# A two-block transformer kernel: shorter way to the first expert routing (columns, root, first head's query)

## The chip, the cores and the metric

One core of a Trainium2 chip runs the whole program. TensorE (PE), VectorE (DVE), ScalarE (ACT), GpSimd (POOL) and SyncE (SP) each run their own list of instructions in order and wait for each other through semaphores. The metric is the device time of one execution in microseconds (µs). TensorE has two clock levels, 1.2 and 2.4 GHz; the profile shows the granted level as a share of the full one, 0.5 or 1.

## What is computed

256 tokens of 1024 features go through two blocks. In the first, attention and a short convolution are mixed and added to x; then 8 heads route every token to 16 of 16384 experts each, and the rows of these experts are gathered from HBM. The second block is a hybrid attention and delta-rule layer. Cut to what the change touches:

```python
x = x + gt1 * (mixed @ w_out[l])
h2 = rmsnorm(x, ln_ffn_g[l]) * (1 + sc2) + sh2
x = x + gt2 * peer_ffn(h2, peer_wq[l], peer_keys[l], peer_u[l], peer_v[l])

# peer_ffn: 8 heads; queries against two sets of 128 keys, the best 16 of each side,
# then the best 16 of their 256 sums give 16 experts and 16 gates g a token
u = expert_u[ec]
act = jax.nn.gelu(jnp.einsum('cd,ced->ce', xc, u).astype(jnp.float32))
return jnp.einsum('ce,ced->cd', gc * act, expert_v[ec])
```

sh2, sc2 and gt2 are parts of the conditioning row `silu(c) @ w_mod + b_mod`.

## The kernel before

The 256 tokens are two tiles (`a` = 0, 1) of 128. All engines' programs are written out by hand: a straight front part, and then one common list of chores, made by `loop_chores`, that each engine walks through, doing its own share of every chore. So the order on every engine is fixed by where a chore stands in that list, and an engine that waits holds back all that stands behind.

Front part, near its end, for tile 0: `attn_mm` multiplies the mixed features with w_out; `attn_add` adds to X; VectorE's `q_norm1` sums the squares of X (L1538) and ScalarE's takes the root (L2110). `mod_cols` on TensorE turns weighted rows of w_mod into columns: the rows m = 0 to 3 are sh2 and sc2 (in RT and rowb), m = 6 and 7 are the second half's gate gt2, which is kept in the rowb row `R_G2`. Every column is a product with one output column, so each loads 128x128 weights for it. VectorE's `mod2` adds the bias. `conv_root(1)` is the root of the convolution's norm for tile 1: TensorE sums squares with ones (L963), ScalarE takes the root (L2191), VectorE's `conv_mix(1)` takes the reciprocal and scales (L1516, L1520). `q_norm2(0)` scales X (L1550, L1552), turns it (L815) and evacuates it with sc2 and sh2 to hT (L1405, L2128). `scores_mm(4)`, `scores_add(4)` belong to the attention of tile 1, whose softmax is spread over the gather. `q_project(0, 0, ..)` makes the queries of heads 0 and 1 from hT and the peer_wq slab (L1016), ScalarE copies them to mixT, `keys` multiplies them with the keys (L1040).

Then the chores. `route(0)` takes heads (0), (1), (2, 3), ... in this order. For each: `top8`, `drop8`, `top16`, `at8`, `at16` on VectorE find the 16 best of both sides, `cand` to `cat16` the best sums, `same`, `pick`, `total`, `expert` the expert numbers. `spread_i` and `spread_g` on TensorE (L1054) spread numbers and gates over the partitions, `take_i` and `take_g` on VectorE take them. `q_back` (L1031) turns hT back to token order for the dot products, and its results are copied to tok2 on ScalarE.

The gather: 128 steps p, two fetches each. One fetch is one indirect DMA from GpSimd (L2474), 268.45 MB in 256 of them, about 1.05 MB each, into one of 8 buffers of AR. At first the buffers 0, 1, 2, 3, 4 and 7 are free for it; every later fetch waits until `accumulate` (L1072) has used the data of its buffer. `dot` on VectorE (L1689) multiplies the first half of the row with the token, `weight` on ScalarE (L2221, L2223, L2106) takes gelu, gate and a diagonal, `accumulate` on TensorE adds the second half. Around them stand pieces of the rest: `scores_mm(5)`, `weigh(4)` (VectorE, L1439, needs ScalarE's exponentials of `scores_add(4)`), routing of the later heads, and for a = 1 the first tile of the second block. After the last fetch the second tile of the second block remains.

A PSUM bank is taken in rotation by `take`; with no event named it is held until `drop`. `S_WQ` are the two peer_wq slabs.

```python
def first_wait(a, h0):
    if h0 == 0:
        return [("idx", 0, 6), ("gwp", 0, 6)] if a else [("mod_cols2", 1)]
```

The first `top8` waits for all columns, since `drop8` writes into the scratch `sw`, which is the same memory as `R_G2`.

## Time and profile before

| | µs |
|---|---|
| median of 3 runs | 1291.72 |
| lowest and highest | 1291.27, 1292.57 |
| the profiled execution | 1300.05 |
| its span in the trace | 1298.2 |

| engine | busy µs | share |
|---|---|---|
| TensorE | 1094.3 | 84% |
| VectorE | 793.2 | 61% |
| ScalarE | 448.3 | 35% |
| GpSimd | 294.0 | 23% |

The profiled execution is 0.6% longer than the median. Shares are means over stages with different limits: a front part (to about 208 µs), the gather (to about 1000 µs) and the rest of the second block. A wait is put down to the event that came last.

### The profile page before, as it was taken

What the parts mean: (1) busy time and instruction counts of PE and PEld (TensorE: products, weight loads), DVE (VectorE), ACT (ScalarE), POOL (GpSimd) and SP (SyncE); (2) the same over time, 40 slices, a digit from 0 to 9 for tenths busy, and PEclk for the clock granted to TensorE, in tenths of its full rate; (3) what the DMA queues carried; (4) which work ended last, traced back from release to release, by engine and by line L of the source; (5) the groups of instructions that cost most, each with busy time, mean ns of one, the idle gap of its engine ahead of it and who ended that gap; (6) DMA issues with size and microseconds to landing.
All of it is one profiled execution on the core that took longest, in us unless ns stands there. A gap on an engine that the chain in (4) does not pass through costs nothing.

```text
span 1298.2 us, 14207 instructions
## 1 busy us (share of the span) xinstructions
PE 1094.3 (84%) x5194; PEld 549.9 (42%) x5194; DVE 793.2 (61%) x1853; ACT 448.3 (35%) x1249; POOL 294.0 (23%) x261
## 2 busy tenths in 40 slices
PE   6989996787887676759897779968999799998998
PEld 2968674333243222213332334423443345555543
DVE  5465756988864999654357667666664367645201
ACT  1113203655442444444253344434334223322201
POOL 0000002434334443433323333333322000000000
PEclk9988967999988889989989989998999799999999
DMA  9995705998999999999999999999999475433573
GB/s 389 326 407 197 275 1 212 366 395 353 421 369 422 421 422 405 405 422 376 422 419 422 421 421 411 421 421 386 391 420 423 196 275 212 178 130 142 217 299 136
DMA packets 63665, 433.16 MB, mean 334 GB/s; under 512 B 6979, under 2 KB 10348, under 8 KB 11884
## 3 DMA queue, kind: packets, MB, share of 16 engines
q0 software_dynamic: 36864, 268.45, 50.7%
q1 hardware_dynamic: 26336, 162.81, 32.2%
q8 instruction: 41, 0.67, 0.2%
q10 hardware_dynamic: 396, 0.99, 0.2%
q14 instruction: 28, 0.23, 0.0%
HBM read 431.17 MB, written 1.06 MB: 333 GB/s over the span
## 4 chain that ended last, share of the span: by engine, by line
PE 55%; DMA 18%; DVE 17%; ACT 6%; issue 2%; POOL 1%; another core or an unknown queue 0%; SPq 0%; POOLq 0%; DVEq 0%; ACTq 0%
PE ps L1117 20%; DMA AR<-in_puv,idx 16%; PE ps L1072 11%; DVE AR L1689 6%; PE ps L766 6%; PE ps L1231 3%; PE ps L988 2%; PE ps L1016 2%; DMA W<-in_w_in 1%; PE ps L801 1%; PE ps L1098 1%; POOL AR L2474 1%; PE ps L935 1%; ACT av L2223 1%; DMA W<-in_w_mod 1%
## 5 line engine op out<-in xcount | busy, mean ns | idle before, releaser
L2474 POOL DMA_INDIRECT AR<-in_puv,idx x256 | 293.7, 1147 | 699.5 <-PE ps L1072 437.2
L1072 PE MATMUL ps<-AR,acc 128*64 128x512 f32 x912 | 288.8, 673 | 115.1 <-ACT acc L2106 112.9
L1689 DVE CUSTOM_DVE_ANT_0 AR<-AR,mixT 128x1024 f32<-128x1024 f32 x128 | 153.1, 1222 | 68.1 <-DMA AR<-in_puv,idx 67.9
L1072 PEld LDWEIGHTS ps<-AR,acc 128*64 128x64 f32 x912 | 72.6, 147 | 284.0 <-ACT acc L2106 187.7
L1117 PE MATMUL ps<-W,AR 128*128 128x512 f32 x416 | 188.7, 596 | 0.7 <-ACT AR L2106 0.7
L1689 DVE CUSTOM_DVE_ANT_0 AR<-AR,tok 128x1024 f32<-128x1024 f32 x128 | 152.8, 1221 | 49.4 <-DMA AR<-in_puv,idx 49.2
L1117 PE MATMUL ps<-W,hT 128*128 128x512 f32 x320 | 160.3, 632 | 2.8 <-DVE PT L1996 2.8
L2221 ACT ACTIVATE av<-av 128x1 f32<-128x1 f32 x256 | 51.4, 201 | 310.6 <-DVE av L1689 306.6
L1117 PEld LDWEIGHTS ps<-W,AR 128*128 128x128 f32 x416 | 75.5, 190 | 77.4 <-issue 75.3
L1117 PEld LDWEIGHTS ps<-W,hT 128*128 128x128 f32 x320 | 58.5, 199 | 77.7 <-issue 72.9
L2106 ACT ACTIVATE acc<-fold,av 128x64 f32<-128x64 f32 x228 | 79.4, 348 | 7.4
L766 PE MATMUL ps<-hT,W 128*128 128x256 f32 x320 | 76.1, 400 | 6.2 <-DMA W<-in_w_in 6.2
L2223 ACT ACTIVATE av<-av,gwp 128x1 f32<-128x1 f32 x256 | 75.6, 295 | 8.3
L766 PEld LDWEIGHTS ps<-hT,W 128*128 128x128 f32 x320 | 64.2, 203 | 16.4 <-issue 6.8
L1072 PE MATMUL ps<-AR,mixT 128*64 128x512 f32 x112 | 44.2, 701 | 21.5 <-ACT mixT L2106 21.3
L2106 ACT ACTIVATE AR<-ps 128x512 f32<-128x512 f32 (+3 forms) x26 | 14.4, 561 | 113.1 <-PE ps L766 57.0
L1974 DVE TENSOR_TENSOR RT<-RT,ps 64x256 f32<-64x256 f32 (+1 forms) x63 | 27.2, 432 | 37.3 <-PE ps L1231 29.4
L2106 ACT ACTIVATE mixT<-ps 128x512 f32<-128x512 f32 (+1 forms) x18 | 9.0, 503 | 81.5 <-PE ps L1016 41.4
L1016 PEld LDWEIGHTS ps<-hT,W 128*128 128x128 f32 x256 | 32.2, 205 | 9.8 <-issue 9.8
L1016 PE MATMUL ps<-hT,W 128*128 128x128 f32 x256 | 34.8, 294 | 0.0
L1117 PE MATMUL ps<-W,tok 128*128 128x512 f32 x64 | 30.7, 620 | 0.0
L2221 ACT ACT_TABLE_LOAD x23 | 29.5, 1283 | 0.4
(449 smaller groups left out, 1317.1 us busy)
## 6 DMA issues: line engine op xcount, KB each, us to landing
W<-in_w_in SPq DMA_DIRECT2D x90, 1024.0 KB, 15.5
W<-in_w_mod SPq DMA_DIRECT2D x24, 1024.0 KB, 14.1
W<-in_wba SPq DMA_DIRECT2D x8, 1024.0 KB
W<-in_wbb SPq DMA_DIRECT2D x8, 1024.0 KB
W<-in_wo SPq DMA_DIRECT2D x8, 1024.0 KB
W<-in_w_out SPq DMA_DIRECT2D x4, 1024.0 KB, 5.9
W<-in_wq SPq DMA_DIRECT2D x4, 1024.0 KB
AR<-in_puv,idx POOLq DMA_INDIRECT x256
```

The source lines that it names most:

```text
L766: t = mm(b[:, o:o + S], slab(i)[:, k, c:c + P], src[:, k, :], start=(k == 0), stop=(k == 7))
L988: t = mm(b[:, :], mixT[:, k, a * P:a * P + P], slab(S_WO[n])[:, k, :], start=(k == 0), stop=(k == 7))
L1016: t = mm(b[:, j * P:j * P + P], slab(S_WQ[m // 2])[:, k, c:c + P], hT[:, k, a * P:a * P + P], start=(k == 0), stop=(k == 7))
L1072: t = mm(of(("E", a, c))[64 * g:64 * g + 64, :], dg_at((2 * p + g) % NDG, late), GB[:, places[g], D + c * 512:D + c * 512 + 512], start=(m ...
L1117: t = mm(b[:, :], src[:, k, :], slab(i)[:, k, :], start=(k == 0), stop=(k == 7))
L1231: t = mm(b[c, q * P + c.start:q * P + c.stop], lhsT[c, q, c], rhs[c, q, c], start=True, stop=True)
L1689: ttr(GB[:, n, 0:D], GB[:, n, 0:D], H2[a][g], 1.0, 0.0, MUL, ADD, av[:, a, c:c + 1]).then_inc(*ve.sig("dot", p, g))
L1974: t = tt(o[c, :, c], o[c, :, c], src[c, :, c], SUB)
L2106: act(dst, src, ACT.Copy, **how).then_inc(*ac.sig(*name))
L2221: t = link(act(w, w, ACT.Gelu_apprx_tanh))
L2223: t = link(act(w, w, ACT.Copy, scale=gwp[:, a, c:c + 1]))
L2474: eng.indirect_dma_start(GB[:, n, :], None, puv, bass.IndirectOffsetOnAxis(ap=idx[:, a, c:c + 1], axis=0)).then_inc(*gp.dma(f"g{n}", "gat" ...
```

## The change

It moves and splits work between the end of the front part and the first gathers. Nothing else of the program differs, and no arithmetic is left out or added but that one projection is made per head.

- `mod_cols` makes only the columns of sh2 and sc2 (16 products instead of 24). The 8 columns of the gate are a chore `gate2`, on TensorE and VectorE, behind the whole routing of head 0. The two weighted rows it reads lie in buffer 7 of AR instead of `R_G2`, so the sixth fetch waits for these products, and `top8` does not.
- ScalarE takes the root of `q_norm1(0)` before that of `conv_root(1)`; TensorE does `conv_root(1)` behind the first head's query.
- `q_first(hd)` and `keys_first(hd)` take the place of `q_project(0, 0)` and its `keys`: one head, one bank a time, so head 0 has its keys before head 1 is projected.
- `scores_mm(4)` stands behind `q_back`; `q_project(0, 1)` and `scores_add(4)` stand behind the routing of head 0.

```diff
-        keys(0)
+        if a:
+            keys(0)
+        else:
+            state["keys"] = 1
...
-    do("q_project", 0, 1, (0, 1))
+    do("scores_mm", 4)
     while (0, 0) not in idx or (0, 0) not in gw:
         advance(routes, 1)
+    do("gate2")
+    do("q_project", 0, 1, (0, 1))
+    do("scores_add", 4)
...
-        sums = [RT[:, 512 * n:512 * n + 512] for n in range(3)] + [R_POST[:, 0:512], R_POST[:, 512:1024], R_LNF[:, 0:512]] + [R_G2[:, 512 * n:512 * n + 512] for n in range(2)]
+        sums = [RT[:, 512 * n:512 * n + 512] for n in range(3)] + [R_POST[:, 0:512], R_POST[:, 512:1024], R_LNF[:, 0:512]] + [ar(14336 + 512 * n, 512) for n in range(2)]
...
+            def q_first(hd):
+                b, old = take(("qf", hd), ("qf", hd))
+                pe.wait_ge(*old, ("w", S_WQ[0]))
+                for k in range(8):
+                    pe.wait_ge(hx(0, k))
+                    t = mm(b[:, 0:P], slab(S_WQ[0])[:, k, hd * P:hd * P + P], hT[:, k, 0:P], start=(k == 0), stop=(k == 7))
+                t.then_inc(*pe.sig("qf_mm", hd))
+            def keys_first(hd):
+                bs = [take(("kf", hd, c)) for c in range(2)]
+                for c in range(2):
+                    pe.wait_ge(*bs[c][1], ("qf", hd), ("keys", 0))
+                    t = mm(bs[c][0][:, hd * P:hd * P + P], qp[c * 64:c * 64 + 64, hd, 0:P], kT_sb[0][c * 64:c * 64 + 64, hd, :],
+                           start=True, stop=True)
+                t.then_inc(*pe.sig("kf_mm", hd))
...
             attn_mm(0, 1)
-            mod_cols()
+            mod_cols("modc2", (0, 1, 2, 3), 0, ("mod2",))
             attn_add(0, 1)
+            q_norm2(0)
+            q_first(0)
             conv_root(1)
-            q_norm2(0)
-            scores_mm(4)
-            q_project(0, 0, (0, 1))
-            scores_add(4)
+            keys_first(0)
+            q_first(1)
+            keys_first(1)
...
             def mod2():
-                ve.wait_ge(("mod_cols2", 1))
+                ve.wait_ge(("mod_cols2", 0))
...
+            def gate2():
+                ve.wait_ge(("mod_cols2", 1))
+                tt(g2c, of("modg")[:, 0:8], PV[:, V_BMOD + 40:V_BMOD + 48], ADD).then_inc(*ve.sig("g2c"))
...
-            conv_root(1)
             q_norm1(0)
             q_norm2(0)
-            q_project(0, 0, (0, 1))
-            scores_add(4)
+            q_first(0)
+            conv_root(1)
+            q_first(1)
...
+                    if n == 7:
+                        gp.wait_ge(("mod_cols2", 1))
```

The rows of the built programs' order give line, operation, tiles (ps is PSUM, K the constants, W a weight slab) and, in brackets, the semaphores waited for; line numbers of the changed kernel are a few higher. First place, TensorE from the columns on, before (L1002 columns, L963 the ones sum, L815 the turn, L935 scores, L1016 queries, L1040 keys):

```order
L1002 MATMUL ps<-K,RT 128x1 x11
L1002 MATMUL ps<-K,rowb 128x1 x12
L963 MATMUL ps<-AR,K 128x128 [waits s_ve_mix]
...
L815 MATMUL ps<-K,tok 128x128 [waits s_ve_norm,s_ac_mix]
...
L935 MATMUL ps<-AR 128x256 x4
L1016 MATMUL ps<-hT,W 128x128 [waits s_ve_h,s_w0,s_ac_mix]
L1016 MATMUL ps<-hT,W 128x128 [waits s_ve_h]
...
L1016 MATMUL ps<-hT,W 128x128 x8
L1040 MATMUL ps<-hT,mixT 128x128 [waits s_in_keys,s_ac_route]
...
L1031 MATMUL ps<-K,hT 64x128 x16
```

and after (L1007 columns, L821 the turn, L1019 the first head's query, L969 the ones sum, L1026 its keys):

```order
L1007 MATMUL ps<-K,RT 128x1 x11
L1007 MATMUL ps<-K,rowb 128x1 x4
L821 MATMUL ps<-K,tok 128x128 [waits s_ve_norm]
...
L821 MATMUL ps<-K,tok 128x128 [waits s_ac_mix]
...
L1019 MATMUL ps<-hT,W 128x128 [waits s_ve_h,s_w0]
L1019 MATMUL ps<-hT,W 128x128 [waits s_ve_h]
L1019 MATMUL ps<-hT,W 128x128 [waits s_ac_h] x2
...
L969 MATMUL ps<-AR,K 128x128 x4
L1026 MATMUL ps<-hT,mixT 128x128 [waits s_in_keys,s_ac_route]
L1026 MATMUL ps<-hT,mixT 128x128
L1019 MATMUL ps<-hT,W 128x128 x8
...
L1054 MATMUL ps<-K,hT 64x128 x24
```

The eight last columns, the ones sum and the scores no longer stand ahead of the first query; the ones sum stands between head 0's query and its keys.

Second place, ScalarE from the first root to the first `weight`, before (L2191 root of the convolution's norm, L2110 root for X, L2106 copies, L2158 exponentials, L2221 gelu):

```order
L2191 ACTIVATE AR<-ps,K 128x128 [waits s_pe_mix] x2
L2110 ACTIVATE st<-st 128x1 [waits s_ve_norm]
...
L2106 ACTIVATE mixT<-ps 128x2x128 [waits s_pe_route]
...
L2158 ACTIVATE rowb,sm<-rowb,sm 128x256 [waits s_ve_attn]
L2158 ACTIVATE rowb,sm<-rowb,sm 128x256 x3
L2106 ACTIVATE tok<-ps 128x512 [waits s_pe_route] x4
L2106 ACTIVATE mixT<-ps 128x2x128 [waits s_pe_route]
L2212 ACTIVATE gw<-gw 128x16 [waits s_ve_route]
...
L2221 ACTIVATE av<-av 128x1 [waits s_dot]
```

and after (the same as L2222, L2141, L2137, L2189, L2256):

```order
L2222 ACTIVATE AR<-ps,K 128x128 [waits s_pe_mix]
L2141 ACTIVATE st<-st 128x1 [waits s_ve_norm]
...
L2137 ACTIVATE mixT<-ps 128x128 [waits s_pe_route]
L2222 ACTIVATE AR<-ps,K 128x128 [waits s_pe_mix]
L2137 ACTIVATE mixT<-ps 128x128 [waits s_pe_route]
L2137 ACTIVATE tok<-ps 128x512 [waits s_pe_route] x4
...
L2247 ACTIVATE gw<-gw 128x16 [waits s_ve_route]
L2137 ACTIVATE mixT<-ps 128x2x128 [waits s_pe_route]
L2189 ACTIVATE rowb,sm<-rowb,sm 128x256 [waits s_ve_attn]
L2189 ACTIVATE rowb,sm<-rowb,sm 128x256 x3
...
L2256 ACTIVATE av<-av 128x1 [waits s_dot]
```

The copy of the queries of heads 2 and 3 and the four exponentials now stand behind the gate's exponential (L2212, now L2247) and right before the gelu of the first gathered rows.

Third place, TensorE around the spreading of head 0's experts, before (L1054 both spreads, L1072 `accumulate`):

```order
L1031 MATMUL ps<-K,hT 64x128 x16
L1031 MATMUL ps<-K,hT 64x128 [waits s_ve_attn]
...
L1016 MATMUL ps<-hT,W 128x128 x16
L1054 MATMUL ps<-RT,K 64x8 [waits s_ve_route,s_ac_route]
...
L1054 MATMUL ps<-gw,K 64x8 [waits s_ve_route,s_ac_route]
...
L1072 MATMUL ps<-AR,mixT 64x512 [waits s_dg,s_ac_route]
```

and after (L1054 `q_back`, L941 scores, L1081 both spreads, L1007 gate columns, L1039 queries of heads 2 and 3, L1099 `accumulate`):

```order
L1054 MATMUL ps<-K,hT 64x128 x24
...
L941 MATMUL ps<-AR 128x256 [waits s_ac_route]
...
L1081 MATMUL ps<-RT,K 64x8 [waits s_ve_route,s_ac_route]
...
L1081 MATMUL ps<-gw,K 64x8 [waits s_ve_route]
...
L1007 MATMUL ps<-K,AR 128x1 x8
L1039 MATMUL ps<-hT,W 128x128 x16
L1099 MATMUL ps<-AR,mixT 64x512 [waits s_dg,s_ve_attn]
```

The queries of heads 2 and 3 moved from ahead of the spreads to behind them, with the gate's eight columns ahead.

## Rows read from the trace of the kernel before

**Rows 1.** Windows: busy µs (instructions) per engine, granted clock, DMA share, GB/s.

```profile
210.00:1000.00 790.00, 636.98 (x2762) 263.32 (x2762) 541.33 (x1298) 333.89 (x989) 292.53 (x255) 0.92 0.99 406
1000.00:1298.00 298.00, 272.35 (x1302) 143.31 (x1302) 129.66 (x283) 72.32 (x163) 0.00 (x0) 0.98 0.53 203
```

**Rows 2.** Timeline of GpSimd: start µs, µs busy, line, operation, idle before and releaser.

```profile
208.52 1.08 POOL L2474 DMA_INDIRECT AR<-in_puv,idx  x1 [207.68 <-DVE gw L1679]
...
221.80 1.55 POOL L2474 DMA_INDIRECT AR<-in_puv,idx  x1 [5.42 <-PE ps L1072]
```

**Rows 3.** Timeline of TensorE, 172 to 223 µs; x counts records: two a product, one a turn.

```profile
172.61 3.05 PE L1002 MATMUL ps<-K,RT 128*128 128x1 f32 x24
175.52 5.26 PE L1002 MATMUL ps<-K,rowb 128*128 128x1 f32 x24
180.64 2.05 PE L963 MATMUL ps<-AR,K 128*128 128x128 f32 x8
184.32 1.94 PE L815 MATMUL ps<-K,tok 128*128 128x128 f32 x8 [1.63 <-DVE tok L1552]
186.19 3.78 PE L935 MATMUL ps<-AR 64*128 64x256 f32 x8
189.90 6.42 PE L1016 MATMUL ps<-hT,W 128*128 128x128 f32 x32
...
197.44 3.71 PE L1031 MATMUL ps<-K,hT 128*64 128x128 f32 x64
201.09 3.84 PE L1016 MATMUL ps<-hT,W 128*128 128x128 f32 x32
...
219.54 3.46 PE L1072 MATMUL ps<-AR,mixT 128*64 128x512 f32 x6 [0.94 <-ACT mixT L2106]
```

**Rows 4.** Timeline of VectorE, 174 to 219 µs.

```profile
174.26 1.22 DVE L1538 CUSTOM_DVE_ANT_0 junk<-X 128x1024 f32<-128x1024 f32 x1
...
180.81 0.17 DVE L1542 TENSOR_TENSOR modc<-ps,PV 128x16 f32<-128x16 f32 x1 [5.32 <-PE ps L1002]
...
183.22 0.16 DVE L1550 RECIPROCAL st<-st 128x1 f32<-128x1 f32 x1 [1.96 <-ACT st L2110]
...
186.51 0.94 DVE L1516 RECIPROCAL AR<-AR 128x128 f32<-128x128 f32 x1
...
188.68 0.68 DVE L1430 TENSOR_TENSOR rowb<-ps,acc 128x512 f32<-128x512 f32 x1
...
190.73 1.22 DVE L1433 TENSOR_REDUCE sm<-rowb 128x4 f32<-128x1024 f32 x1
...
197.57 0.50 DVE L1577 MAX8 RT<-ps 128x8 f32<-128x128 f32 x2 [5.56 <-PE ps L1040]
...
218.46 0.17 DVE L1439 RECIPROCAL sm<-sm 128x4 f32<-128x4 f32 x1
```

**Rows 5.** Timeline of ScalarE, 182 to 220 µs.

```profile
182.73 0.37 ACT L2191 ACTIVATE AR<-ps,K 128x128 f32<-128x128 f32 x1 [25.00 <-PE ps L963]
...
185.44 1.66 ACT L2128 ACTIVATE hT<-ps,modc 128x128 f32<-128x128 f32 x4 [2.26 <-PE ps L815]
196.35 0.38 ACT L2106 ACTIVATE mixT<-ps 128x256 f32<-128x256 f32 x1 [9.25 <-PE ps L1016]
...
198.05 0.51 ACT L2158 ACTIVATE rowb<-rowb,sm 128x256 f32<-128x256 f32 x1
...
205.47 1.28 ACT L2221 ACT_TABLE_LOAD   x1
...
219.14 0.35 ACT L2106 ACTIVATE mixT<-fold,av 128x64 f32<-128x64 f32 x1
```

**Rows 6.** Windows of one or two µs at three changes of the granted clock.

```profile
195.00:196.00 1.00, 1.00 (x9) 1.00 (x9) 0.00 (x0) 0.00 (x0) 0.00 (x0) 0.83 0.00 0
209.00:210.00 1.00, 0.00 (x0) 0.00 (x0) 0.00 (x0) 0.00 (x0) 0.69 (x2) 0.50 0.00 0
222.00:224.00 2.00, 2.00 (x7) 0.96 (x6) 2.00 (x8) 1.09 (x5) 1.70 (x2) 0.84 1.00 422
```

More of the change, by code:

```diff
@@ L49 @@
     "pe_mix": ("ones_mm", "o_mm"),
-    "pe_route": ("qp_mm", "h2_mm", "keys_mm", "spread_mm"),
+    "pe_route": ("qp_mm", "qf_mm", "h2_mm", "keys_mm", "kf_mm", "spread_mm"),
     "pe_proj": ("proj", "bd_mm"),
@@ L79 @@
     "ac_mix": ("osq", "aroot", "croot"),
-    "ac_route": ("qp", "h2", "gexp"),
+    "ac_route": ("qp", "qf", "h2", "gexp"),
     "ac_x2": ("x2_sq", "x2_root", "g2"),
@@ L993, in attn_add, with mod_cols @@
                 drop(("o", a, n), ("x1_gate", a, n))
-            def mod_cols():
-                b, old = take("modc2", ("mod2",), ("g2c",))
+            def mod_cols(use, ms, n, freed):
+                b, old = take(use, freed)
                 pe.wait_ge(*old, "K")
-                for m in (0, 1, 2, 3, 6, 7):
-                    c = 4 * m if m < 4 else 4 * m - 8
+                for i, m in enumerate(ms):
                     pe.wait_ge(("mods", m))
                     for j in range(4):
-                        t = mm(b[:, c + j:c + j + 1], sums[m][:, j * P:j * P + P], ones[:, 0:1], start=True, stop=True)
-                    if m == 3:
-                        t.then_inc(*pe.sig("mod_cols2", 0))
-                t.then_inc(*pe.sig("mod_cols2", 1))
+                        t = mm(b[:, 4 * i + j:4 * i + j + 1], sums[m][:, j * P:j * P + P], ones[:, 0:1], start=True, stop=True)
+                t.then_inc(*pe.sig("mod_cols2", n))
+            def gate2():
+                mod_cols("modg", (6, 7), 1, ("g2c",))
+            def q_first(hd):
[12 more added lines that the diff above has]
+                t.then_inc(*pe.sig("kf_mm", hd))
             def q_project(a, m, js):
@@ L1044, in at8 @@
             def at8(a, h0, nh, hd, c):
-                if hd % 2 == 1 and c == 1:
+                if a == 0 and hd < 2:
+                    if c == 1:
+                        for c in range(2):
+                            drop(("kf", hd, c), ("at8", 0, hd, 1))
+                elif hd % 2 == 1 and c == 1:
                     for c in range(2):
@@ L1328, in tensor @@
             attn_mm(0, 1)
-            mod_cols()
+            mod_cols("modc2", (0, 1, 2, 3), 0, ("mod2",))
             attn_add(0, 1)
+            q_norm2(0)
+            q_first(0)
             conv_root(1)
-            q_norm2(0)
-            scores_mm(4)
-            q_project(0, 0, (0, 1))
-            scores_add(4)
-            parts = {"keys": keys, "q_back": q_back, "q_project": q_project, "spread_i": spread_i, "spread_g": spread_g,
+            keys_first(0)
+            q_first(1)
+            keys_first(1)
+            parts = {"keys": keys, "q_back": q_back, "q_project": q_project, "gate2": gate2, "spread_i": spread_i, "spread_g": spread_g,
                      "accumulate": accumulate, "scores_mm": scores_mm, "turn_p": turn_p, "pv": pv, "cmp_s1": cmp_s1,
@@ L1565, in first_wait @@
                 if h0 == 0:
-                    return [("idx", 0, 6), ("gwp", 0, 6)] if a else [("mod_cols2", 1)]
+                    return [("idx", 0, 6), ("gwp", 0, 6)] if a else [("mod_cols2", 0)]
                 return [("expert", a, 0 if h0 == 1 or a and h0 == 2 else 1 if h0 == 2 else h0 - 2)]
             def part(a, hd, c):
-                return key_part([of("ks", a, hd // 2, 0), of("ks", a, hd // 2, 1)], hd, c)
+                use = ("kf", hd) if a == 0 and hd < 2 else ("ks", a, hd // 2)
+                return key_part([of(*use, 0), of(*use, 1)], hd, c)
             def left(hd, c):
@@ L1575, in top8 @@
             def top8(a, h0, nh, hd, c):
-                ve.wait_ge(("keys_mm", a, hd // 2), *first_wait(a, h0))
+                ve.wait_ge(("kf_mm", hd) if a == 0 and hd < 2 else ("keys_mm", a, hd // 2), *first_wait(a, h0))
                 routed(vmax(v16[:, hd, c, 0:8], part(a, hd, c)), "top8", a, hd, c)
@@ L2198, in q_norm2, with q_first @@
                          ["mod2_sc"] + ([("keys_mm", 0, 3)] if a else []), lambda k: hx(a, k))
+            def q_first(hd):
+                ac.wait_ge(("qf_mm", hd), ("o_mm", 0, 1))
+                copy(qp[:, hd, 0:P], of("qf", hd)[:, 0:P], "qf", hd)
             def q_project(a, m, js):
@@ L2439, in scalar @@
             conv_root(0)
-            conv_root(1)
             q_norm1(0)
             q_norm2(0)
-            q_project(0, 0, (0, 1))
-            scores_add(4)
+            q_first(0)
+            conv_root(1)
+            q_first(1)
             parts = {"q_back": q_back, "q_project": q_project, "gexp": gexp, "weight": weight, "scores_add": scores_add,
```

4 lines of the change are left out of this document (2 added, 2 removed).

## The prediction

> **What bounds the kernel now.** I read the windows first, then who waits at the seam between the front part and the gather. From 210 to 1000 µs the DMA engines are busy 99% of the time [rows 1]: this long stage goes by the bytes of 256 gathers and the weight slabs, and VectorE (541 of 790 µs) and TensorE have room on the mean. From 1000 µs on TensorE is busy 272 of 298 µs and the slab loads are light; that stretch starts when the gathers end. GpSimd sits idle for the first 207.68 µs and issues the first gather at 208.52 [rows 2]. So the time has a hard seam: whatever comes earlier at the first gather comes earlier at the end, as long as the DMA engines then stay fed. The chain to it is read backward from the rows on TensorE, VectorE and ScalarE [rows 3 to 5]: gate and norm columns, ones sum, root, turn, scores, queries, keys, routing of head 0.
>
> **Columns and root.** Before, 24 column products are 48 records: the first 24 take 3.05 µs, the last 24 take 5.26, since the clock fell to 1.2 GHz among them [rows 3]; 0.127 and 0.219 µs a record. With 32 records, the last 8 at 0.219, they end at 175.5 + 1.75 = 177.3 and not at 180.8: 3.5 µs. VectorE's bias and scale take 0.4 µs (from 180.81). The reciprocal at 183.22 waited for the root, which stood on ScalarE behind the convolution's, so behind 2.05 µs of ones sum [rows 3, 4, 5]; X's squares were summed at 175.5 (174.26 and 1.22), so now the root is ready first. Reciprocal at 177.75, and from there to the turn were 1.10 µs (183.22 to 184.32): turn at 178.85, **5.5 µs earlier**. The change adds no wait here.
>
> **First query.** The turn takes 1.94, to 180.8. The scores (3.78) no longer stand in between: the query begins right there, not at 189.90. ScalarE's four copies to hT (1.66) start about a microsecond after the turn and are used third, fourth, seventh and eighth; I charge nothing for them, at most 0.5. Head 0 alone is 16 records of the 32 that took 6.42 and 3.84 µs [rows 3]: 0.235 a record at 1.2 GHz (the last microsecond of the 6.42 was fast, 195 to 196 in rows 6), 0.12 at 2.4; so 3.8 or 1.9. Then the ones sum, 2.05 or about 1.1. Then ScalarE's root 0.37, and VectorE from the reciprocal at 186.51 to the end of `fold` at 188.68, 2.17, and 0.1 for the last small scaling. Head 0's keys wait for a copy of at most 0.38 and take less than 0.7 (from the copy's end at 196.73 to `q_back` at 197.44 for twice as much), beside that VectorE work and more than 1 µs ahead of its end. So `top8` starts at 180.8 + 3.8 + 2.05 + 0.4 + 2.3 = 189.4 with all of it at 1.2 GHz, at 186.5 with all at 2.4. It started at 197.57 [rows 4]: 8.2 or 11.0 µs. Which level? In this stretch before, TensorE started at 184.3 and was granted 2.4 GHz only past 195; at the first `accumulate` it started at 219.54 and had it between 222 and 224 [rows 6]. I take the rise at about the end of the query, four to six µs in: **9.0 µs**.
>
> **Routing.** From `top8` to the first issue are 10.95 µs of small VectorE operations, unchanged; first issue at **199.5**. What TensorE must have done before the spreading at about 198: head 1's query 1.9, its copy and keys 0.8, `q_back` 3.71, scores 1.9 at the fast level: done at 194.5. The cover is 3.5 µs at 2.4 GHz; without it, see the slower rival. ScalarE's table load (1.28, [rows 5]) ahead of the gate's exponential falls into its idle time. VectorE's `scores_add(4)` (0.68 twice and 1.22) moves from ahead of the keys, where it was hidden, into the wait for the first gather, about 5 µs: again nothing. SyncE's queue is untouched. The sixth fetch now waits for the gate columns; it was issued some 6.4 µs after the first, and the columns take 2.0 to 3.5: nothing.
>
> **What comes back.** ScalarE now has, ahead of the first `weight`: the copy of the queries of heads 2 and 3, four exponentials and a table load; and the copy waits for TensorE's gate columns and that projection. From the first issue at 199.6: columns 2.0 to 3.5 (16 records), projection 3.84 to 7.5 (32 records), copy 0.4, exponentials 2.05 (0.51 each), table 1.28, two `weight`s 1.9 (one took 1.0, from 218.46 to 219.49 in rows 4 and 5), first product 2.3 at 1.2 GHz (219.54 to the issue at 221.80) or 1.2 at 2.4. TensorE stands still from 194.5 to 198. Before, it ran almost nothing from 204.9, the end of the second projection, and was at 0.5 in the window from 209 [rows 6]. So I take the columns at the low level and the projection in part: 3.5 + 6.1. The exponentials end at 211.7, the diagonals at 214.9, the seventh gather is issued at 216.1. Its deadline: six gathers of 1.05 MB at 422 GB/s last 14.9 µs, and it was issued 13.3 µs after the first [rows 2], 1.6 in time. Now the deadline is 214.4: **1.7 µs of empty DMA**. VectorE waits too: `weigh(4)` came to its turn at 218.46, 9 earlier is 209.5, and its exponentials come at 211.7: 2.2 µs, with the routing of head 1 and later dot products queued behind it. Both stalls are one delay seen from two engines, not to be added: I take **2.0**. All fast, they are 0; all slow (first issue at 200.4) the seventh is issued at 219.5 against 215.3: 4.2.
>
> The Trainium skill (TensorE: Matmul & The Clock Gate, HAM oscillation) says that a pause of TensorE lets the clock fall and that the next burst begins at half rate, which speaks against the gap that the change opens before the columns; the row at 209 agrees, and by it alone the stall stays, while without it the sum would be 9. The Trainium skill (DMA: Bandwidth & Descriptors, Specifications) gives a limit of about 358 GB/s for one core's HBM traffic; by it six gathers last 17.6 µs, there is no empty DMA, and the sum would lie between 7 and 9. The row with 422 GB/s disagrees, and the row decides.
>
> **Sum.** 9.0 - 2.0 = 7.0 µs. In the profiled execution 1298.2 becomes about 1291.2; it is 0.6% longer than the median, which changes a term of 7 µs by nothing. 1291.7 - 7.0 = **1284.7 µs**.
>
> **Rivals.**
> - *No stall.* The projection and columns run at 2.4 GHz, or TensorE warms up earlier in the query. Then the shift of 9 to 11 stays whole: 1280.7 to 1282.7. For it: the level has been seen to return within 3 to 4.5 µs. Against: the idle gap.
> - *Slow level at both places, short of the spreading.* 8.2 - 4.2 = 4.0: 1287.7. For it: the 11 µs that the rise took from 184.3.
> - *The shift is soaked up, or the first route isn't what the change brings forward.* The early gathers are then paced by VectorE's routing and dots (69% busy over the stage, more at its start), and idle DMA time there grows by what was won: 1291.7. Against: 99% DMA share.
> - *Slower: TensorE stays at 1.2 GHz from 175 into the gather.* Place: `q_back` and the scores, ahead of the spreading. Head 1's query ends at 191, with copy and keys 192.2, `q_back` 7.4, scores 3.8: 203.4, so the spreading is 4.5 late and the first issue is at 204.9. Then 11.0 + 0.4 + 2.05 + 1.3 + 1.9 + 2.3 puts the seventh gather at 223.9, past the 221.8 of today by more than its slack of 1.6; and each of the first pairs costs TensorE about 4 µs of products and 4 of scores or turns against 5 µs of gathering, 3 more for one or two pairs: plus 3 to 5, 1294.7 to 1296.7. It decides when 2.4 GHz has not come by about 199. Against it: TensorE works almost without a gap from 178.9.
>
> **How the numbers follow.** Forecast (1282.7 to 1287) 0.48, no stall 0.18, slow level 0.18, soaked up 0.09, slower 0.07. The range reaches over the first three: 1281.0 to 1289.3. 0.2% is 2.6 µs, about what a measurement of this kernel can tell from no change: faster means under 1289.1, which takes nearly all of the first three, 0.83; within 0.10; slower 0.07.
>
> **What would show it.** In the trace after: 16 column records at each place; the turn near 178.9; `top8` near 188.6; the first indirect DMA near 199.5 (8.2 to 11 earlier than 208.52); the exponentials of `scores_add(4)` ending near 211.7 and VectorE idle before `weigh(4)` for about 2 µs; the seventh gather near 216 and a window there with a DMA share below 1; the last gather about 7 earlier than before; everything behind it of the same length. It is wrong if the first issue shifts and the last does not, or if TensorE reaches the spreading later than VectorE's `expert`.

## Result and the profile after

The changed kernel takes 1287.48 µs at the median of 6 runs (1284.58 to 1289.6), the kernel before 1292.14 (6 runs, three of them those of the table above): 4.7 µs less by the two medians. The estimated ratio of the two kernels, which is not the quotient of these medians, is 0.9958, 95% interval 0.9943 to 0.9974; on 1292 that is 5.4 µs less, between 3.4 and 7.4. A second set of runs of both gave 1286.54 against 1293.72, 7.2 less by the medians, and a ratio of 0.9951 (0.9928 to 0.9974), 6.3 less. The forecast was 7.0 less; the time lies in its range. The profiled execution has a span of 1287.8 µs.

**TensorE after**, from the columns to the first accumulation (as [rows 3]):

```profile
170.75 1.45 PE L994 MATMUL ps<-W,mixT 128*128 128x512 f32 x3
172.03 2.91 PE L1007 MATMUL ps<-K,RT 128*128 128x1 f32 x24
174.81 1.85 PE L1007 MATMUL ps<-K,rowb 128*128 128x1 f32 x8
177.98 1.97 PE L821 MATMUL ps<-K,tok 128*128 128x128 f32 x8 [1.33 <-DVE tok L1583]
179.75 2.68 PE L1019 MATMUL ps<-hT,W 128*128 128x128 f32 x16
182.26 1.06 PE L969 MATMUL ps<-AR,K 128*128 128x128 f32 x8
183.25 0.49 PE L1026 MATMUL ps<-hT,mixT 64*128 64x128 f32 x4
...
197.28 3.57 PE L1007 MATMUL ps<-K,AR 128*128 128x1 f32 x16
200.72 5.93 PE L1039 MATMUL ps<-hT,W 128*128 128x128 f32 x32
211.40 4.26 PE L1099 MATMUL ps<-AR,mixT 128*64 128x512 f32 x8 [4.75 <-ACT mixT L2137]
```

The attention product ends at 172.20. Then come 32 column records, the turn, head 0's query (16 records) straight behind it, the ones sum, head 0's keys. The gate columns and the projection of heads 2 and 3 stand at 197.28 to 206.65, beside the first six fetches. **VectorE after** (as [rows 4]):

```profile
176.69 0.17 DVE L1570 TENSOR_TENSOR modc<-ps,PV 128x16 f32<-128x16 f32 x1 [1.77 <-PE ps L1007]
...
176.98 0.15 DVE L1581 RECIPROCAL st<-st 128x1 f32<-128x1 f32 x1
177.17 0.76 DVE L1583 TENSOR_SCALAR tok<-X,st 128x1024 f32<-128x1024 f32 x1
...
183.75 0.95 DVE L1544 RECIPROCAL AR<-AR 128x128 f32<-128x128 f32 x1 [3.47 <-ACT AR L2222]
184.74 1.14 DVE L1548 SCALAR_TENSOR_TENSOR mixT<-AR,PV 128x128 f32<-128x128 f32 x4
...
186.00 0.48 DVE L1609 MAX8 RT<-ps 128x8 f32<-128x128 f32 x2
...
209.06 0.18 DVE L1467 RECIPROCAL sm<-sm 128x4 f32<-128x4 f32 x1 [1.21 <-ACT rowb L2189]
```

The norm's reciprocal no longer waits for the root. But the first MAX8 has no idle time in front of it: it doesn't wait for the keys (ready at 183.74), it stands behind the convolution's mixing, which began at 183.75, after 3.47 µs of waiting for the convolution's root. **ScalarE** (as [rows 5]) **and GpSimd** (as [rows 2]) after:

```profile
183.36 0.37 ACT L2222 ACTIVATE AR<-ps,K 128x128 f32<-128x128 f32 x1 [0.62 <-PE ps L969]
...
206.69 0.38 ACT L2137 ACTIVATE mixT<-ps 128x256 f32<-128x256 f32 x1 [14.29 <-PE ps L1039]
206.97 0.50 ACT L2189 ACTIVATE rowb<-rowb,sm 128x256 f32<-128x256 f32 x1
...
209.05 1.28 ACT L2256 ACT_TABLE_LOAD   x1
...
211.71 0.35 ACT L2137 ACTIVATE mixT<-fold,av 128x64 f32<-128x64 f32 x1
```

```profile
197.13 1.08 POOL L2511 DMA_INDIRECT AR<-in_puv,idx  x1 [196.28 <-DVE gw L1711]
...
214.74 0.93 POOL L2511 DMA_INDIRECT AR<-in_puv,idx  x1 [10.31 <-PE ps L1099]
```

The first fetch comes at 197.13 (before 208.52), the seventh 17.6 µs behind it (before 13.3): it waits 10.31 µs for the first accumulation. **Windows after**, first the two stages of [rows 1], then the start of the gather, then single microseconds around the first accumulation:

```profile
210.00:1000.00 790.00, 633.76 (x2778) 262.24 (x2780) 542.69 (x1299) 335.64 (x997) 286.72 (x250) 0.94 0.99 405
1000.00:1288.00 288.00, 266.58 (x1288) 141.43 (x1284) 125.09 (x275) 70.25 (x155) 0.00 (x0) 0.98 0.52 197
```

```profile
210.00:220.00 10.00, 8.60 (x28) 3.48 (x28) 9.90 (x30) 3.61 (x13) 2.16 (x3) 0.83 0.83 316
220.00:230.00 10.00, 4.96 (x18) 1.81 (x18) 8.31 (x23) 8.86 (x25) 3.98 (x4) 0.95 0.96 369
230.00:240.00 10.00, 8.71 (x40) 4.24 (x38) 8.32 (x19) 2.99 (x10) 4.04 (x4) 0.88 0.84 308
...
211.00:212.00 1.00, 0.60 (x2) 0.19 (x2) 1.00 (x8) 0.94 (x4) 0.00 (x0) 0.99 0.97 410
212.00:213.00 1.00, 1.00 (x4) 0.51 (x4) 1.00 (x2) 0.05 (x1) 0.00 (x0) 0.50 1.06 442
```

In the ten microseconds from 210 the DMA engines were idle 1.7 µs (share 0.83), in those from 230 another 1.6. The second hole isn't the change's doing: the kernel before has one about as far behind its first fetch (share 0.88 from 240 to 250, 1.2 µs), and so has the version ring below (0.90 and 0.88 from 220 to 230 in its two traces).

**All versions in one table.** A trace's start and TensorE's clock wander by some microseconds from one execution to the next, so every time is counted from an event on the path: the end of the last attention product on TensorE (172.77 in the kernel before), the start of the normed tokens on VectorE (`tok`), the first MAX8, the first, the seventh and the last of the 256 fetches.

| version | product to tok | tok to MAX8 | MAX8 to first fetch | first to seventh | first to last |
|---|---|---|---|---|---|
| before | 10.65 | 14.15 | 10.95 | 13.3 | 784.6 |
| before_again | 7.66 | 13.89 | 10.96 | 13.3 | 784.0 |
| root_alone | 6.38 | 14.20 | 10.95 | 13.4 | 783.7 |
| after | 4.97 | 8.83 | 11.13 | 17.6 | 788.3 |
| after_again | 5.10 | 8.70 | 11.14 | 17.6 | 788.6 |
| cols_back | 4.59 | 11.85 | 10.93 | 15.4 | 788.6 |
| heads_back | 3.99 | 10.56 | 11.14 | 19.0 | 786.3 |
| root_back | 5.19 | 7.28 | 10.96 | 18.7 | 789.4 |
| scores_back | 4.97 | 16.63 | 11.15 | 14.1 | 784.0 |
| delay | 3.99 | 18.83 | 11.16 | 18.3 | 785.4 |
| ring | 3.98 | 8.83 | 11.15 | 13.1 | 784.2 |
| ring_again | 3.98 | 8.69 | 11.15 | 13.0 | 784.1 |
| ring_root | 5.19 | 7.33 | 10.95 | 13.1 | 786.3 |
| ring_mix | 5.00 | 6.59 | 10.95 | 12.5 | 786.4 |

From the product to the first fetch: 35.75 and 32.51 µs before, 24.93 and 24.94 after. So the fetches start 7.6 to 10.8 µs earlier, and take 3.7 to 4.6 longer. The middle of the first, 9.2, less the middle of the second, 4.1, is 5.1 µs; 5.4 and 6.3 were timed. That it comes so close is partly luck: the two traces of before alone differ by 3.2 µs at the first fetch.

### The profile page after: what moved, and what is told of

Same layout as the page of the kernel before. It is cut to its first block, busy times and chain, and to the rows that moved or that the text cites. A ratio compares the mean times of both kernels' runs of the same rounds, so it can differ in the third digit from the quotient of the medians.

```text
span 1287.8 us, 14205 instructions
## 1 busy us (share of the span) xinstructions
PE 1083.2 (84%) x5194; PEld 545.9 (42%) x5194; DVE 793.2 (62%) x1853; ACT 448.4 (35%) x1250; POOL 292.8 (23%) x261
## 3 DMA queue, kind: packets, MB, share of 16 engines
HBM read 431.17 MB, written 1.06 MB: 336 GB/s over the span
## 4 chain that ended last, share of the span: by engine, by line
PE 51%; DMA 21%; DVE 18%; ACT 5%; issue 2%; POOL 1%; SPq 0%; POOLq 0%; DVEq 0%; ACTq 0%
PE ps L1144 20%; DMA AR<-in_puv,idx 18%; PE ps L1099 10%; DVE AR L1721 7%; PE ps L772 6%; PE ps L1258 3%; PE ps L994 2%; DMA W<-in_w_mod 2%; POOL AR L2511 1%; DMA W<-in_w_in 1%; PE ps L1125 1%; PE ps L1039 1%; PE ps L877 1%; DVE rowb L1866 1%; ACT av L2258 1%
## 5 line engine op out<-in xcount | busy, mean ns | idle before, releaser
L1099 PE MATMUL ps<-AR,acc 128*64 128x512 f32 x912 | 286.4, 664 | 114.0 <-ACT acc L2137 112.6
L1099 PEld LDWEIGHTS ps<-AR,acc 128*64 128x64 f32 x912 | 71.6, 146 | 282.3 <-ACT acc L2137 188.2
L1144 PE MATMUL ps<-W,hT 128*128 128x512 f32 x320 | 157.6, 623 | 4.0 <-DVE PT L2028 3.9
L2256 ACT ACTIVATE av<-av 128x1 f32<-128x1 f32 x256 | 51.2, 200 | 301.6 <-DVE av L1721 301.3
L2137 ACT ACTIVATE acc<-fold,av 128x64 f32<-128x64 f32 x228 | 79.3, 348 | 7.4
L772 PEld LDWEIGHTS ps<-hT,W 128*128 128x128 f32 x320 | 64.0, 202 | 15.6 <-issue 6.1
L1099 PE MATMUL ps<-AR,mixT 128*64 128x512 f32 x112 | 40.2, 658 | 18.5 <-ACT mixT L2137 18.3
L2137 ACT ACTIVATE AR<-ps 128x512 f32<-128x512 f32 (+3 forms) x26 | 14.4, 561 | 112.2 <-PE ps L772 56.0
L2137 ACT ACTIVATE mixT<-ps 128x512 f32<-128x512 f32 (+2 forms) x19 | 9.2, 485 | 86.9 <-PE ps L1039 44.8
L1039 PEld LDWEIGHTS ps<-hT,W 128*128 128x128 f32 x224 | 28.7, 208 | 9.7 <-issue 9.7
L1039 PE MATMUL ps<-hT,W 128*128 128x128 f32 x224 | 31.0, 297 | 0.0
## 6 DMA issues: line engine op xcount, KB each, us to landing
W<-in_w_mod SPq DMA_DIRECT2D x24, 1024.0 KB, 13.3
```

Of the source, the lines that this page charges most:

```text
L772: t = mm(b[:, o:o + S], slab(i)[:, k, c:c + P], src[:, k, :], start=(k == 0), stop=(k == 7))
L1039: t = mm(b[:, j * P:j * P + P], slab(S_WQ[m // 2])[:, k, c:c + P], hT[:, k, a * P:a * P + P], start=(k == 0), stop=(k == 7))
L1099: t = mm(of(("E", a, c))[64 * g:64 * g + 64, :], dg_at((2 * p + g) % NDG, late), GB[:, places[g], D + c * 512:D + c * 512 + 512], start=(m ...
L1144: t = mm(b[:, :], src[:, k, :], slab(i)[:, k, :], start=(k == 0), stop=(k == 7))
L2137: act(dst, src, ACT.Copy, **how).then_inc(*ac.sig(*name))
L2256: t = link(act(w, w, ACT.Gelu_apprx_tanh))
```

## Experiments

The theory to be tested: the time has a hard seam at the first fetch; the change brings it forward, and part of that is lost at once, since the seventh fetch waits for a chain over TensorE's gate columns and projection and ScalarE's copy, exponentials and table load. The rivals: the shift is soaked up in the gather whatever comes; or the gather is longer for another reason than this chain.

**The two kernels once more.** Neither is edited.

> The changed kernel itself, again, for a closer interval and a second trace. Theory 1 (the first gather comes 9 to 11 us earlier, and 2 to 4 us of that are given back in the first twenty microseconds of the gather, because ScalarE's first weight stands behind the copy of the queries of heads 2 and 3 and four exponentials): 0.9945 of before (-7 us), the seventh indirect DMA over 14.9 us after the first, as in the first trace (17.6). Rival (the whole shift is soaked up bit by bit by the routing and dot products of the next hundred microseconds): -3 us or less, and the last gather less than 4 us earlier than before.

> The kernel before, a second look. The stretch from the end of the attention product to the first indirect DMA, 35.75 us in the first trace, should differ from it by up to 2 us with where the clock falls among the columns (root_alone had 48 column records in 6.2 us, the first trace in 8.2); the fetches 1 to 256 should take 784 to 785 us again.

The changed kernel repeats itself to 0.1 µs at the seams: 24.94 to the first fetch, +17.6 to the seventh. The kernel before does not: 32.51 instead of 35.75. Its second 24 column records took 2.82 µs, not 5.26 as in [rows 3]:

```profile
174.45 2.82 PE L1002 MATMUL ps<-K,rowb 128*128 128x1 f32 x24
177.13 1.82 PE L963 MATMUL ps<-AR,K 128*128 128x128 f32 x8
```

The windows in which the granted clock fell from 1.00 to 0.50 (2.4 to 1.2 GHz), in the first trace of the kernel before and in this one:

```profile
174.00:175.00 1.00, 1.00 (x11) 1.00 (x10) 0.97 (x2) 0.00 (x0) 0.00 (x0) 0.93 0.00 0
```

```profile
177.00:178.00 1.00, 1.00 (x8) 1.00 (x8) 0.42 (x3) 0.00 (x0) 0.00 (x0) 0.70 0.00 0
```

It fell about 2.1 µs behind the attention product in the first and 5.4 behind it in the second, with the same instructions in the same order. So 3 µs of the difference between the first traces of before and after is where that fall happened to land. This execution took 1285.83 µs, 6 to 9 less than the medians of its kernel; a single time says little here.

**A delay ahead of the first MAX8.** The changed kernel with eight reductions more on VectorE, just ahead of the first MAX8:

```diff
             ts(gnh[:, :], PV[:, V_GN:V_GN + 1], 0.5, None, MUL).then_inc(*ve.sig("gnh"))
+            for _ in range(8):
+                ve.wait_ge(link(red(osq[:, 15:16], X[:, 0, :], AX, ADD)))
```

> The changed kernel with eight reductions of a 128x1024 tile on VectorE (some 9.5 us) right ahead of the first top8; their result is used by nothing. If the seam is hard, the time is 8 to 9.5 us above the changed kernel's, about 2 to 3 us above before; a little less than the delay, since the gate's columns and the queries of heads 2 and 3 still wait for the routing. If shifts at the seam are soaked up, it is within 4 us of the changed kernel.

Timed 1296.20 µs against 1286.54 for the changed kernel in the same comparison, 9.7 more (ratio to the kernel before 1.0016, 0.9992 to 1.0039); the MAX8 came 9.0 later (22.82 from the product, in the changed kernel 13.80). By the two ratios (1.0016 and 0.9951) it is 8.4 more. So a microsecond at this seam is about a microsecond of the time, and the rival that the shift is soaked up (within 4 µs of the changed kernel) is out. The one trace says less: its last fetch is 6 µs later behind the product than in the changed kernel, since its gather took 785.4 and not 788.3; a third of the delay was won back there, and whether that is so in every execution isn't shown.

**The cause of the longer gather.** In the version ring, VectorE's addition and sums of the scores of tile 4 go ahead of the gate columns' addition, and ScalarE's copy of the projection of heads 2 and 3 becomes a step of its own behind the first `weight`. So the exponentials wait neither for the gate columns nor for the projection:

```diff
-    do("gate2")
-    do("q_project", 0, 1, (0, 1))
     do("scores_add", 4)
+    do("gate2")
+    do("q_project", 0, 1, (0, 1))
...
-        yield [("weigh", 4), ("scores_mm", 5)]
+        yield [("q_copy", 0, 1), ("weigh", 4), ("scores_mm", 5)]
```

> The changed kernel, but scores_add(4) stands ahead of the gate's columns, and ScalarE copies the queries of heads 2 and 3 only behind the first pair's weight. TensorE's order is that of the changed kernel. Theory 1: the seventh indirect DMA comes 13.3 us after the first as before the change, VectorE does not wait at weigh(4), the DMA share from 210 to 220 us is 1, and the time is 2.5 to 4 us below the changed kernel's (0.992 of before). Rival (the gather's pace is VectorE's, which the stall does not set): the seventh fetch moves but the last one does not, and the time is that of the changed kernel.

> ring as it was, on the same chip as ring_mix. Theory: the first MAX8 again 8.83 us behind the normed tokens' start, first fetch at 23.9 to 25.0 from the attention product's end according to how many of the first 32 column products ran at TensorE's lower granted clock, seventh fetch at +13.1, and 3 to 4 us less than the changed kernel, 9 less than the kernel before. Rival, that the stall had gone by luck: seventh fetch at +17.

ScalarE, GpSimd and two windows in ring:

```profile
194.97 1.08 POOL L2515 DMA_INDIRECT AR<-in_puv,idx  x1 [194.12 <-DVE gw L1711]
...
197.91 0.51 ACT L2189 ACTIVATE rowb<-rowb,sm 128x256 f32<-128x256 f32 x1 [7.69 <-DVE sm L1461]
...
200.00 1.28 ACT L2260 ACT_TABLE_LOAD   x1
...
208.04 0.94 POOL L2515 DMA_INDIRECT AR<-in_puv,idx  x1 [5.11 <-PE ps L1099]
```

```profile
210.00:215.00 5.00, 4.11 (x15) 1.20 (x13) 4.50 (x15) 2.03 (x6) 2.05 (x2) 1.00 1.01 423
215.00:220.00 5.00, 3.49 (x11) 1.60 (x13) 4.86 (x13) 4.12 (x11) 1.35 (x1) 0.66 1.02 428
```

The exponentials start 2.9 µs behind the first fetch instead of 9.8, the seventh fetch is at +13.1, the DMA engines have no hole from 210 to 220 (nor from 10 to 20 µs behind the first fetch), and the gather is back at 784.2. Timed: 1283.24, ratio 0.9929 (0.9904 to 0.9953), 3.3 µs less than the changed kernel beside it; and again 1283.11, 0.9909 (0.9886 to 0.9932). Two traces of each version agree, so the chain was the cause in the changed kernel. How the lateness is carried on can be read from the 24th fetch, before and after:

```profile
270.17 0.94 POOL L2474 DMA_INDIRECT AR<-in_puv,idx  x1 [0.30 <-issue]
```

```profile
262.88 0.94 POOL L2511 DMA_INDIRECT AR<-in_puv,idx  x1 [0.31 <-issue]
```

It comes 61.7 µs behind the first fetch before and 65.8 after (61.5 in ring). The seventh was 4.3 later than before, the 24th 4.1, the last 3.7: the lateness goes nearly whole through the gather, though the DMA engines were idle for only 2.0 µs from 10 to 30 µs behind the first fetch, and for none before.

**Parts of the change, each by itself.** root_alone is the kernel before with one thing of the change, ScalarE's norm root ahead of the convolution's (`conv_root(1)` behind `q_norm1(0)` in ScalarE's list). root_back is the changed kernel without that part: the convolution's second root ahead of the turn on TensorE, and ahead of the norm's root on ScalarE.

```diff
             attn_add(0, 1)
+            conv_root(1)
             q_norm2(0)
             q_first(0)
-            conv_root(1)
             keys_first(0)
...
             conv_root(0)
+            conv_root(1)
             q_norm1(0)
             q_norm2(0)
             q_first(0)
-            conv_root(1)
```

> The kernel before with one part of the change: ScalarE takes the root for X ahead of that of the convolution's norm. By the trace of before the reciprocal at 183.22 can then start at 181.3, when the modulation columns are done: the turn and the first gather 2 us earlier, counted from the end of the attention product. If the columns and not the root were what it waited for, nothing moves.

> The changed kernel with the convolution's ones sum ahead of the turn again and its root ahead of X's root. By the trace the turn then comes at the end of the columns and the ones sum, 1.1 to 2.05 us less the 1.3 us of idle TensorE, and the root another 0.6 us behind it: the turn 1.5 to 3 us later. But the convolution's root is then done before the query, and VectorE's 2.3 us of scaling lie beside TensorE's query instead of behind it: top8 starts when the keys are done, 13.8 + 2 - 2.3, so at about the same 13.5 to 14.5 us. If the root were worth what I charged for it, top8 would be 2 us later or more.

Alone, the root's order makes the reciprocal start right behind the columns' addition (from the product to `tok` 6.38 instead of 7.66, though its columns ended 0.5 later: worth 1.8, where 2 was expected). Its one execution took 1287.64 µs. Taken out of the changed kernel, it makes `tok` wait for the root, 1.11 µs; and yet the MAX8 comes earlier, 12.47 from the product instead of 13.80. TensorE and VectorE in root_back:

```profile
177.41 0.16 DVE L1581 RECIPROCAL st<-st 128x1 f32<-128x1 f32 x1 [1.11 <-ACT st L2141]
...
180.71 0.94 DVE L1544 RECIPROCAL AR<-AR 128x128 f32<-128x128 f32 x1
...
184.23 0.61 PE L1026 MATMUL ps<-hT,mixT 64*128 64x128 f32 x4 [0.37 <-ACT mixT L2137]
...
184.89 0.50 DVE L1609 MAX8 RT<-ps 128x8 f32<-128x128 f32 x2 [1.87 <-PE ps L1026]
```

The mixing now runs at 180.71, while TensorE is at the query, and the MAX8 waits 1.87 µs for the keys and for nothing else. From `tok` to the MAX8 it is 7.28 µs instead of 8.83. So the change's new place for the convolution's root saves 1.1 ahead of the turn and costs 1.4 to 1.5 behind it. The columns also ran 1.0 µs faster in this execution, which is in the 12.47; `tok` to MAX8 is free of that, though its query took 3.62 µs and not 2.68, since the clock rose later. Net of the columns the root's move costs 0.3 to 0.4 µs, too little for the time to show. ring_root, the same edit made on ring, repeats it:

> ring with the convolution's root back where the kernel before has it: on TensorE ahead of the turn, on ScalarE ahead of the norm's root. Theory: the normed tokens wait for the root (1.7 us behind the columns' end, in ring 0.6), but the first MAX8 then waits for TensorE alone and comes 7.3 us behind the normed tokens' start (ring 8.8), so it comes 0.4 us earlier than in ring, 12.4 from the attention product's end with 8 of 32 columns at the lower clock: the root's move gained nothing where the mixing stays ahead of the MAX8. Rival, that the root's move was worth its 1.1 us: the MAX8 at 13.9 from the attention product's end.

7.33 from `tok` to the MAX8, 12.52 from the product, seventh fetch at +13.1. One execution each gave 1285.32 (root_back) and 1282.23 (ring_root), within about 2 µs of the versions that they were made from: these two rest on the traces, not on the time.

heads_back puts the projection of heads 0 and 1 together, with their keys as a pair, in place of head 0 alone; cols_back puts the 16 gate column records back between the other columns and the turn:

```diff
             q_norm2(0)
-            q_first(0)
+            q_project(0, 0, (0, 1))
             conv_root(1)
-            keys_first(0)
-            q_first(1)
-            keys_first(1)
```

```diff
             mod_cols("modc2", (0, 1, 2, 3), 0, ("mod2",))
+            mod_cols("modg", (6, 7), 1, ("g2c",))
             attn_add(0, 1)
```

> The changed kernel with the queries and keys of heads 0 and 1 made in one piece again ahead of the first top8, the ones sum between queries and keys. 16 records more ahead of the ones sum: top8 1.9 us later at 2.4 GHz, 3.8 at 1.2, so 15.7 to 17.6 us after the attention product and not 13.8.

> The changed kernel with the gate's eight columns back ahead of the turn (16 records). The turn waits for them: 16 records at 0.13 to 0.22 us less the 1.3 us that TensorE idled ahead of the turn, so top8 1 to 2.2 us later than 13.8 us after the attention product. The stall of the gather gets smaller by the 3.5 us of columns that no longer stand behind the routing: the seventh fetch 14 to 15 us after the first and not 17.6. So nearly the same time as the changed kernel: the part moves its cost from one side of the seam to the other. If the rival is right, that the stall does not matter, it is 1 to 2 us slower.

In heads_back `tok` to MAX8 is 10.56, 1.7 µs more than in the changed kernel (1.9 was expected); from the product it is 14.55 and not the 15.7 expected, as its columns ran 1.0 µs faster. Its rows say why it is later:

```profile
178.29 4.42 PE L1036 MATMUL ps<-hT,W 128*128 128x128 f32 x32
182.55 1.06 PE L966 MATMUL ps<-AR,K 128*128 128x128 f32 x8
183.54 0.72 PE L1060 MATMUL ps<-hT,mixT 64*128 64x128 f32 x8
...
184.04 0.95 DVE L1534 RECIPROCAL AR<-AR 128x128 f32<-128x128 f32 x1 [5.21 <-ACT AR L2212]
```

The keys of both heads are done at 184.26, the MAX8 starts at 186.28: here too it waits for the mixing. A query of 16 records instead of 32 pays because the ones sum stands behind it, not because the keys come earlier. That it pays in the time isn't shown: the last fetch of this one trace is 812.0 µs behind the product, in the changed kernel 813.3. In cols_back `tok` to MAX8 is 11.85, 3.0 µs more: the turn waits for the columns' end at 180.35, and the query behind it takes 3.62 µs, not 2.68, as the clock rose later; the MAX8 is 16.44 behind the product, 2.6 more, where 1 to 2.2 was expected. Its seventh fetch is at +15.4 instead of +17.6, since the gate columns are out of the chain; the length of its gather, 788.6, doesn't show that gain. One execution each gave 1283.86 and 1286.63.

scores_back puts the scores of tile 4 back ahead of the first query on TensorE, and their addition and sums behind the mixing on VectorE:

```diff
             q_norm2(0)
+            scores_mm(4)
             q_first(0)
             conv_root(1)
             keys_first(0)
```

> The changed kernel with the scores of tile 4 (8 products of TensorE, VectorE's addition and sums) back ahead of the first query, as in the kernel before. Theory, a row moves everything behind it on the path: 8 products of 64x256 are put between the turn and the first query, 3.78 us as in the kernel before, so the first MAX8 comes 3.7 us later than in the changed kernel, at 17.5 from the attention product's end, the first fetch at 28.6; the stall stays or shrinks a little (seventh fetch at +16.5 to +17.6), since the exponentials still stand behind the copy of the second projection. Rival, that they find room in TensorE's waits: 13.8 and 24.9 as before.

The MAX8 came 7.8 µs later, not 3.7:

```profile
180.27 3.78 PE L939 MATMUL ps<-AR 64*128 64x256 f32 x8
183.98 3.78 PE L1017 MATMUL ps<-hT,W 128*128 128x128 f32 x16
187.55 1.51 PE L967 MATMUL ps<-AR,K 128*128 128x128 f32 x8
...
191.68 1.28 DVE L1458 TENSOR_TENSOR rowb<-ps,acc 128x512 f32<-128x512 f32 x2
193.00 1.22 DVE L1461 TENSOR_REDUCE sm<-rowb 128x4 f32<-128x1024 f32 x1
```

3.7 of it are the scores, 1.5 the query and the ones sum (5.3 µs at mostly 1.2 GHz against 3.7), 2.5 the addition and sums, which stand ahead of the MAX8. In return the exponentials were long done at the first fetch, the seventh was at +14.1, and the gather took 784.0. It took 1289.72 µs in its one execution. So by this one trace moving the scores is the largest part of the change, 7.8 µs, and it is the same move that hangs the exponentials into the chain of the seventh fetch, 4.

**The mixing off the path.** ring_mix is ring with VectorE's mixing of the convolution's second half behind head 0's routing:

```diff
+    do("conv_mix", 1)
     do("scores_add", 4)
     do("gate2")
...
             q_norm2(0)
-            conv_mix(1)
             fold_ident()
```

> The version ring with one more move: VectorE's mixing of the convolution's second half (the reciprocal and four products, 0.95 and 1.14 us, that stand between the turn and the first MAX8) goes behind head 0's routing, ahead of the scores of tile 4. Theory, from the runs so far: in the changed kernel and in ring the first MAX8 does not wait for TensorE's product with the keys (its end 181.56 in ring) but for that chain (MAX8 at 183.82, at the end of a chain that began 3.47 us late because the root came late). So the MAX8 comes 2.2 us earlier, at 10.6 us from the end of the attention product's last product (ring 12.8, changed kernel 13.8) and the first fetch at 21.8 (ring 24.0); the seventh fetch stays within 0.5 us of +13.1. The time falls by 2 us against ring where the attention product ends at the same time. Rival, that the MAX8 waits for TensorE in any case: the first fetch stays at 24.0. Second rival, that 2.1 us more of VectorE work ahead of the exponentials' sums brings the stall back: seventh fetch at +14 or later, and the time of ring.

```profile
185.34 0.50 DVE L1610 MAX8 RT<-ps 128x8 f32<-128x128 f32 x2 [3.27 <-PE ps L1027]
...
208.80 0.94 POOL L2515 DMA_INDIRECT AR<-in_puv,idx  x1 [4.74 <-PE ps L1100]
```

`tok` to MAX8 is 6.59, 2.24 less than in ring, as expected; the MAX8 waits for TensorE's keys. From the product it is 11.59, not 10.6, as its columns took 1.0 µs longer at the lower clock, and the first fetch is at 22.5, not 21.8. The seventh fetch is at +12.5. Timed 1280.66 µs, ratio 0.9891 (0.9868 to 0.9914), 2.5 less than ring beside it by the medians, but the intervals overlap, and in its one trace the gather took 2.3 µs longer than in ring: the gain at the first fetch is shown, that in the time isn't clear of noise. It beats the kernel before by 14 µs, and the changed one by 6 (medians) or 8 (ratios); these are of different comparisons, each against the kernel before.

## Why the prediction was right, and where it was off

- *The bound.* Right: the window from 210 to 1000 has a DMA share of 0.99 as before, and the run with the delay carried 9.0 µs at the seam to 8.4 (ratios) or 9.7 (medians) of the time.
- *Columns and root, 5.5 µs.* The turn started 11.55 µs behind the product before and 5.78 after, 5.8 earlier. But against the second trace of the kernel before (8.56) it is 2.8. The term was worked out from one execution, in which the clock had fallen as early as in any of the 14 traces (they range from 2.1 to 5.4 µs behind the product; the changed kernel's two are at 2.1 and 2.2); the step took that fall for a property of the kernel. The list of signs has a slip, 16 column records at each place: it is 32 ahead of the turn, as the sum says, and 16 behind the routing.
- *First query, 9.0 µs in all.* From the turn to the MAX8 I worked out 9.75 µs; it was 8.0. TensorE was granted 2.4 GHz again within the window from 181 to 182, some 3 µs behind the turn's start and not four to six, at the query's end, so the query took 2.68 and not 3.8 µs, the ones sum 1.06 and not 2.05. Together the MAX8 came 11.0 earlier than in the first trace of before, the upper end of the working, and 7.75 earlier than in the second, under its lower end of 8.2. So the 9.0 is near the middle by the luck of where the clock fell and rose. That VectorE's mixing, not the keys, ends last was in the sum as a chain of 2.3 µs. What I didn't see is that this chain is late only because the change puts the convolution's root behind the query.
- *Routing.* Right: 11.13 instead of 10.95, TensorE done at 192.1 and idle 3.24 µs ahead of the spreading. The slower rival, a TensorE that is late for the spreading, was far off.
- *What comes back, 2.0 µs.* The mechanism was right and its first half was met closely: gate columns 3.57 and projection 5.93 µs (taken 3.5 and 6.1), exponentials' end 11.9 µs behind the first fetch (12.2), and 1.7 µs of idle DMA from 210 to 220 (1.7); VectorE waited 1.21 µs ahead of `weigh(4)`, about half of the 2.2. The term itself was too small, since the gather got 4.1 µs longer. Two things were missing. The first accumulation ran at 1.2 GHz: after TensorE's 4.75 µs of waiting the clock was still at 0.99 when it began and fell at 212, so the eight records took 4.26 µs and the seventh fetch came at +17.6, not at +16.6. That alone would have made the working's hole 2.7 µs and not 1.7, so the 1.7 met is luck. And the term charged only the idle time of the DMA engines, with 1.6 µs of slack taken off; the runs show the whole lateness of the seventh fetch against before, 4.3 µs, still there at the 24th, 4.1, and at the last, 3.7, with 2.0 µs of idle DMA. Why the slack did not count isn't shown. The 4.1 are near the 4.2 that I had worked out for the case with everything at 1.2 GHz, by another way.
- *The sum.* 7.0 forecast, 5.4 and 6.3 timed: a shift of about 9, as taken, less 4.1 instead of 2.0. The term of what comes back is the one that was mis-sized. The first fetch shifted by 11.4 in the profiled executions, a little past the 8.2 to 11 of the signs, and the last by 7.7 (about 7 forecast); counted from the product, the last fetch is 7.1 earlier than in the first trace of before and about 3 earlier than in the second.

The Trainium skill (TensorE: Matmul & The Clock Gate, HAM oscillation) says that a pause lets the clock fall and that the next burst begins at half rate; the trace after agrees at the gate columns, which began at 0.50 at 197.28, behind a pause from 192.1 to 195.4 in which the level fell. At the first accumulation it agrees only in part: that burst began at 0.99, and the level fell 0.6 µs into it. The windows of this kernel show 405 GB/s over 790 µs after, and 423 in ring from 210 to 215; and in the trace after the hole from 210 was there, 1.7 µs. The Trainium skill (HBM Reference, Specifications (TRN2)) says that 358 GB/s, the figure weighed in the prediction, is one core's share while both cores of a pair stream, and that a core alone measures about 425; on this one core the trace agrees with the latter.

## What to carry to other kernels

When work is moved off the path to a seam, look for who needs that work next: here the scores' exponentials, moved out of the way of the first fetch, stood in front of the seventh. Two reorderings, the exponentials ahead of the projection's copy and the mixing behind the routing, gave another 6 to 8 µs together; only the first, 3.3 by the medians, is clear of noise by itself. And when one chain is shortened, ask at its end which other chain now arrives last; a part that helped by itself (the root's order) can cost once the others are in, here by the traces 0.3 to 0.4 µs. A term that rests on the clock level in one trace needs a second trace, or both ends.
